# Merging the put-back of expert pairs by token tile, with a new map of scratch places, in a four-layer decoder trunk

## The chip, the cores and the metric

The kernel runs on one core of one Trainium2 chip. The metric is the device time of one launch in microseconds. Every layer of the model is in this one launch.

## What is computed

The input is 256 tokens of 1024 features in float32. Four layers follow each other; layer i takes mixer i mod 3 (short convolution, retention, spatial gating), so layers 0 and 3 have the convolution, layer 1 the retention and layer 2 the gating. After its mixer every layer normalizes, runs the experts, normalizes again, and adds a gated embedding:

```python
for i in range(DEPTH):
    mix = (conv, retention, sgu)[i % 3](x)
    x = _layer_norm(ALPHA * x + mix, ln_g[i, 0], ln_b[i, 0])
    ffn = _moe(x, router_w, router_b, moe_w_gate[i], moe_w_up[i], moe_w_down[i])
    x = _layer_norm(ALPHA * x + ffn, ln_g[i, 1], ln_b[i, 1])
    x = x + sigmoid(x @ ple_w_gate[i] + ple_b_gate[i]) * (p[i] @ ple_w_proj[i])
```

`_moe` picks 2 of 16 experts for each token and sums `combine[:, e] * ((silu(h @ w_gate[e]) * (h @ w_up[e])) @ w_down[e])` over the experts. The expert weights of a layer are 16 x 3 x 1024 x 512 float32, about 100 MB.

## The kernel before

**Two kinds of work for the TensorE.** A dense stage (mixer, gate) multiplies with weights that are split in two parts: a slot of 1 MB (128 partitions x 2048 float32) is loaded into one of six `raw` places, ScalarE writes its high part (`w_hi`, L1249), VectorE the rest (`w_lo`, L1557), and three matmuls use them (L642 to L644). An expert stage multiplies the gathered tokens with unsplit expert weights (L1034).

**The expert stage.** A layer's 16 experts are 8 pairs p of two. Each expert has room for 64 tokens, 32 from each of the two token tiles t. For a pair the TensorE gathers the tokens (L1026), multiplies by four slots of gate weights, four of up and, in the next pair's turn, four of down (`wide`, `down`, 8 matmuls L1034 for a slot). So a layer has 96 loads k of 1 MB in a fixed order (`expert_stream`). Of pair 0 the gate is k 0 to 3 and the up is k 4 to 7. In pair 1 the gate is k 8 to 11; after it come the transpose of pair 0's hidden rows (`turn`), the transpose of its own places (`turn_pick`, L1104) and the gathers for a later pair (`more`), and only then up, k 12 and 13. `more` waits for `place_ready` before its second half. The last load is k 95.

**Put-back.** The outputs of pair p (128 rows: 2 experts x 64 tokens) are evacuated by ScalarE (high part) and VectorE (rest) in `save_y`, one instruction of 128x512 each for either half c of the columns. `put(p)` adds them to the tokens' rows: for each tile t, each half c and both parts one matmul L1044 with the pair's 0/1 matrix `place_of(p)` (`save_place`, VectorE) as weights. That is 8 matmuls a pair and 64 a layer. Pairs 3 to 6 (`LATER`) keep their outputs in places of their own; only the four matmuls of tile 0 run at once, the four of tile 1 at the end (`put_later`), while VectorE already normalizes tile 0. Outputs of the four pairs lie in `w_hi` 1 to 3 and in `xT_hi`.

**The load queue.** All loads of weights are issued by the sync engine in one order that is written out in the code; if one waits, all behind it wait. A dense slot (L479) waits until the slot that was in its place has been used. An expert load (L525) waits in `wait_place`. Expert weights go to any place that is free by then: `expert_places` gives each k a place. There are 22 first places (k 0 to 21), among them the six `raw`, four `high`, four in the arena that the mixers work in (`work`), two `spare`, and `bias`, `norm`, `x`, `y`, `xg`, `emb`. Three of these serve once in a layer (`xg` for k 3, `y` for k 9, `emb` for k 10); the other 19 form a ring: each later k takes the place whose last load is the oldest, and waits for that load's last matmul. So k 22 follows k 0, and from k 30 on a load follows the one 19 before it (k 30 waits for k 11, k 31 for k 12). The ring loses a place when pair 3's outputs need it, and two more with pairs 4 and 5.

`BEHIND` says after which dense slots of a mixer the first expert loads are queued. The keys count the slots from the start of the mixer; the values are numbers of loads. What is not queued there follows after the mixer's last slot. In layer 1 the mixer has 32 slots, in layer 2 it has 36, in the others 16.

```python
BEHIND = [{8: 1, 9: 1, ..., 13: 1, **more} for more in ({14: 2, 15: 3}, {27: 3, 31: 1}, {27: 2, 31: 2, 35: 1})]
```

The norm's parameters lie in `ln_par`, which is the place `norm`; so an expert load can go there only after the first norm of the layer.

## Time and profile before

| | us |
|---|---|
| median of 3 runs | 1613.21 (1612.29 to 1614.31) |
| the profiled execution, its own time | 1616.79 |
| span of the profile, from the first to the last instruction | 1614.9 |
| busy PE (matmul) | 1597.1 (99%) |
| busy DVE (VectorE) | 684.0 (42%) |
| busy ACT (ScalarE) | 460.7 (29%) |
| moved by the weight queue | 530.93 MB, 81.2% of the DMA engines' span |

Busy time is summed over the whole launch. It says nothing on which of two things that run side by side ends last at a given place. The chain of waits and the stretches of time do.

### The profile page before, as it was taken

How to read it: one execution, taken by the hardware profiler on the slowest of the kernel's cores; microseconds unless marked ns; L12 is line 12 of the kernel's file. 1: busy time of each engine (PE TensorE's matmuls, PEld its weight loads, DVE VectorE, ACT ScalarE, POOL GpSimd, SP SyncE). 2: the span in 40 equal slices, each digit the busy share in tenths (PEclk: the TensorE clock that was granted, in tenths of full speed). 3: DMA queues.
4: the chain of work that ended last, by engine and by line, in shares of the span. 5: the costliest groups of instructions: out<-in, count | busy, mean ns of one | idle time of the engine just before them, and what ended most of it. 6: DMA issues, size and time to landing. Idle time of an engine off the chain costs nothing.

```text
span 1614.9 us, 17974 instructions
## 1 busy us (share of the span) xinstructions
PE 1597.1 (99%) x7568; PEld 956.4 (59%) x7568; DVE 684.0 (42%) x1059; ACT 460.7 (29%) x557; POOL 46.2 (3%) x47
## 2 busy tenths in 40 slices
PE   9999999999999999999999999999999999999998
PEld 7874433478877744333788888643434887444335
DVE  5671111294757711111957755511115767211117
ACT  5522111154433221111544433211102552211113
POOL 1000000010000000000110000000010000000000
PEclk9999999999999999999999999999999999999999
DMA  6999999946636799999557556999997388999992
GB/s 260 367 372 407 422 421 420 421 169 264 242 133 242 281 420 421 421 420 421 213 189 293 180 205 235 384 396 421 421 420 327 134 345 369 395 422 421 421 421 100
DMA packets 75146, 534.41 MB, mean 331 GB/s; under 512 B 8976, under 2 KB 9264, under 8 KB 10544
## 3 DMA queue, kind: packets, MB, share of 16 engines
q1 hardware_dynamic: 73728, 530.93, 81.2%
q0 software_dynamic: 1328, 2.21, 0.4%
q8 instruction: 65, 1.06, 0.3%
q14 instruction: 25, 0.20, 0.0%
HBM read 532.06 MB, written 1.05 MB: 330 GB/s over the span
## 4 chain that ended last, share of the span: by engine, by line
PE 88%; DMA 6%; DVE 5%; issue 1%; ACT 1%; SPq 0%; DVEq 0%; ACTq 0%
PE psum L1034 37%; PE psum L642 12%; PE psum L644 12%; PE psum L643 12%; PE psum L1026 4%; DMA raw<-in_experts 4%; PE psum L1044 3%; PE psum L653 3%; DVE w_lo L1557 2%; PE psum L987 2%; DMA x<-in_experts 2%; PE psum L980 1%; PE psum L793 1%; PE psum L932 1%; PE psum L877 1%
## 5 line engine op out<-in xcount | busy, mean ns | idle before, releaser
L1557 DVE TENSOR_TENSOR w_lo<-raw,w_hi 128x2048 fp32r<-128x2048 f32 (+1 forms) x128 | 272.2, 2143 | 191.0 <-ACT w_hi L1249 190.6
L642 PE MATMUL psum<-w_hi,xT_hi 128*128 128x512 f32 x672 | 265.1, 394 | 3.0 <-DVE w_lo L1557 3.0
L1249 ACT ACTIVATE w_hi<-raw 128x2048 fp32r<-128x2048 f32 (+1 forms) x128 | 221.6, 1752 | 160.9 <-PE psum L644 109.8
L644 PE MATMUL psum<-w_hi,xT_lo 128*128 128x512 f32 x672 | 261.8, 390 | 0.0
L643 PE MATMUL psum<-w_lo,xT_hi 128*128 128x512 f32 x672 | 261.6, 389 | 0.0
L1249 ACT ACTIVATE work<-psum 128x512 f32<-128x512 f32 x152 | 85.8, 597 | 344.6 <-PE psum L653 247.3
L642 PEld LDWEIGHTS psum<-w_hi,xT_hi 128*128 128x128 f32 x672 | 126.2, 188 | 30.2 <-DVE w_lo L1557 3.5
L1034 PE MATMUL psum<-raw,xg 128*64 128x512 f32 x624 | 143.8, 594 | 0.0
L644 PEld LDWEIGHTS psum<-w_hi,xT_lo 128*128 128x128 f32 x672 | 126.1, 188 | 26.6
L643 PEld LDWEIGHTS psum<-w_lo,xT_hi 128*128 128x128 f32 x672 | 126.2, 188 | 25.8 <-issue 0.2
L1557 DVE TENSOR_TENSOR work_r<-psum,work_r 128x512 fp32r<-128x512 f32 x52 | 34.5, 688 | 184.9 <-ACT work_r L1249 184.9
L1954 DVE TENSOR_REDUCE cg<-psum 128x1 f32<-128x256 f32 x32 | 13.6, 425 | 233.8 <-PE psum L1104 233.8
L1249 ACT ACTIVATE xg<-psum 128x512 f32<-128x512 f32 x84 | 49.8, 597 | 200.6 <-PE psum L653 102.4
L1034 PE MATMUL psum<-expert_work,xg 128*64 128x512 f32 x448 | 103.5, 594 | 0.0
L1034 PE MATMUL psum<-raw,work 128*64 128x512 f32 x400 | 93.5, 594 | 2.8 <-DMA raw<-in_experts 2.8
L1034 PEld LDWEIGHTS psum<-raw,xg 128*64 128x64 f32 x624 | 43.9, 137 | 84.2 <-issue 83.9
L642 PE MATMUL psum<-w_hi,work_r 128*128 128x512 f32 x224 | 89.3, 398 | 0.8 <-ACT work L1249 0.8
L644 PE MATMUL psum<-w_hi,work_r 128*128 128x512 f32 x224 | 87.6, 391 | 0.0
L643 PE MATMUL psum<-w_lo,work_r 128*128 128x512 f32 x224 | 87.6, 391 | 0.0
L1034 PE MATMUL psum<-expert_high,xg 128*64 128x512 f32 x336 | 79.5, 594 | 0.0
L1557 DVE TENSOR_TENSOR w_hi<-psum,w_hi 128x512 fp32r<-128x512 f32 x24 | 16.6, 692 | 141.6 <-ACT w_hi L1249 141.6
L1249 ACT ACTIVATE work_r<-psum 128x512 fp32r<-128x512 f32 x52 | 29.4, 600 | 161.4 <-PE psum L1034 157.9
(169 smaller groups left out, 1696.9 us busy)
## 6 DMA issues: line engine op xcount, KB each, us to landing
raw<-in_experts SPq DMA_DIRECT2D x128, 1024.0 KB, 16.7
raw<-in_slots SPq DMA_DIRECT2D x120, 1024.0 KB, 4.9
expert_work<-in_experts SPq DMA_DIRECT2D x88, 1024.0 KB, 16.1
expert_high<-in_experts SPq DMA_DIRECT2D x60, 1024.0 KB, 12.6
expert_spare<-in_experts SPq DMA_DIRECT2D x40, 1024.0 KB, 13.7
expert_bias<-in_experts SPq DMA_DIRECT2D x20, 1024.0 KB, 14.5
x<-in_experts SPq DMA_DIRECT2D x20, 1024.0 KB, 16.7
expert_norm<-in_experts SPq DMA_DIRECT2D x16, 1024.0 KB, 14.4
```

The costliest lines, as they stand in the source:

```text
L642: mm(out, lhs[0], rhs[0], start=start, stop=False)
L643: mm(out, lhs[0], rhs[1], start=False, stop=False)
L644: return mm(out, lhs[1], rhs[0], start=False, stop=stop)
L653: last = nc.tensor.transpose(psum[:, bank, i * P:(i + 1) * P], c, ident[:, :])
L793: last = mm(bank, x_whole[:, 2 * at + j, 0:P], w[:, 2 * j + c, :], start=start, stop=stop)
L877: last = mm(psum[:, 4 + k % 4, :], sT[:, h, (c + s) * P:(c + s + 1) * P], rv[:, s, h * DV:(h + 1) * DV], start=s == 0, stop=s == c)
L987: last = mm(psum[:, 2 * t + c, :], pT[:, j, t * P:(t + 1) * P], whole[:, 2 * j + c, :], start=j == 0, stop=j == 1)
L1026: last = mm(rows_of(psum[:, bank, j * SEQ:(j + 1) * SEQ], t, 4), x_split[a][:, t, chunk], pick[:, t, Q * P:(Q + 1) * P], start=a == 0, sto ...
L1034: last = mm(psum[columns(e), bank, :], lhs(j, e), w[:, 2 * j + e, :], start=start and j == 0, stop=stop and j == 1)
L1044: last = mm(psum[:, bank0 + 2 * t + c, :], where[:, t * P:(t + 1) * P], what[i][:, c * NB:(c + 1) * NB], start=start and i == 0, stop=stop ...
L1249: return nc.scalar.activation(dst, src, func)
L1557: return tt(lo, whole, hi.bitcast(F), ALU.subtract)
```

## The change

Pairs 0 and 1, 2 and 3, 4 and 5 are merged two by two. The pair of either parity writes its outputs and its 0/1 rows so that one tensor of 128 rows holds the four experts' 32 rows of tile 0, and another those of tile 1. `put` then runs at odd p only: for pairs 0 and 1 it does both tiles (8 matmuls), for 2 and 3, 4 and 5 tile 0 at once and tile 1 at the end (4 and 4). Pair 6 (4 and 4) and pair 7 (8) stay as they were. The new `save_y` evacuates an even pair whole into both tensors (two instructions where there was one) and an odd pair in four pieces of 32 rows (four where there was one), on ScalarE and on VectorE. The 0/1 matrix of an odd pair is added to that of the even pair by a SCALAR_TENSOR_TENSOR in place of a TENSOR_SCALAR. The two halves of a pair's outputs now use banks 6 and 7, and the TensorE's wait between them goes.

The scratch arrays of the expert stage get a place for each kind of mixer, so that the mixers free other parts of the arena first. `spare` 0 now takes one load of a layer and is then the home of the merged tile 1 outputs. `norm` is free after the layer before; the first norm's parameters go to scratch and are loaded late in the mixer. The load order puts `spare`, `spare`, `norm`, `bias` first, and 13 places instead of 11 (in layer 1 instead of 10) are queued among the mixer's slots. There are still 22 first places; four of them (`spare` 0, `xg`, `y`, `emb`) serve once, so that the ring has 18: k 30 follows k 12 and k 31 follows k 13. Only `high` 1 is taken out of the ring later.

```diff
-LATER = range(3, 7)
-BEHIND = [{8: 1, 9: 1, 10: 1, 11: 1, 12: 1, 13: 1, **more} for more in ({14: 2, 15: 3}, {27: 3, 31: 1}, {27: 2, 31: 2, 35: 1})]
+BEHIND = [{5: 3, 7: 1, 8: 1, 9: 1, 10: 1, 11: 1, 12: 1, 13: 1, 15: 3},
+          {1: 3, 5: 1, 8: 1, 9: 1, 10: 1, 27: 3, 30: 2, 31: 1},
+          {1: 3, 5: 1, 8: 1, 9: 1, 10: 1, 27: 2, 31: 3, 35: 1},
+          {1: 3, 5: 4, 8: 1, 9: 1, 10: 1, 15: 3}]
...
-        ring = [("bias", 0), ("spare", 0), ("spare", 1), raw[4], raw[5], high[0], *early, raw[3], tail[0], raw[0], tail[1], raw[1], tail[2], *late,
-                ("norm", 0), raw[2], ("x", 0)]
...
-        given_up = {high[i + 1]: AT[p, "down", 1] for i, p in enumerate(LATER[:3])}
+        work, xg, y = [("work", i) for i in range(4)], ("xg", 1), ("y", 0)
+        free = [("spare", 0), ("spare", 1), ("norm", 0), ("bias", 0)]
+        dense = [raw[4], raw[5], high[0]]
+        first = [[*free, *work[:3], *dense, xg, work[3], y],
+                 [*free, *dense, *work[:2], xg, *work[2:], y],
+                 [*free, *dense, work[0], xg, *work[1:], y]][layer % 3]
+        order = [*first, raw[3], tail[0], raw[0], tail[1], raw[1], tail[2], raw[2], ("x", 0), ("emb", 0)]
+        n_first = len(order)
+        once = {("spare", 0): 0, xg: EARLY_K, y: LATE_K, ("emb", 0): LAST_K}
+        turns = iter([k for k in range(n_first) if k not in once.values()])
+        loads = [once[place] if place in once else next(turns) for place in order]
+        at = dict(zip(loads, order))
+        ring = [place for place in order if place not in once]
+        last = {at[k]: k for k in loads if at[k] in ring}
+        given_up = {high[1]: AT[4, "down", 1]}
...
+def output_parts(p):
+
+    everything = slice(0, P)
+    if p >= MERGED:
+        return [(everything, 0)]
+    if p % 2 == 0:
+        return [(everything, t) for t in range(T)]
+    return [(slice(CAP * q, CAP * (q + 1)), (q + 1) % 2) for q in range(4)]
...
         def outputs(L, p, t):
+            if p == MERGED:
                 home = xT[0][:, :, :].rearrange("p j n -> p (j n)")
+            elif p > MERGED or t == 0:
+                return scratch[L % 3].y
             else:
-                home = w_hi[:, 1 + LATER.index(p), :]
...
+        def place_of(L, p):
+
+            m = scratch[L % 3]
+            return m.place if p < 2 or p == PAIRS - 1 else m.kept[p // 2 - 1]
...
                 elif kind == "spare":
-                    if L:
+                    if L and i == 0:
+                        sp.wait_ge(ffn_done, T * L)
+                    elif L:
                         sp.wait_ge(experts_used, last_use(L - 1, ("spare", i)))
                 elif kind == "norm":
-                    sp.wait_ge(x_tile_ready, 6 * L + 2)
+                    if L:
+                        sp.wait_ge(x_tile_ready, 6 * L - 2)
                 elif kind == "x":
                     sp.wait_ge(x_lo_ready, T * (L + 1))
...
-                elif L % 3 == 0 and i < 3:
-                    sp.wait_ge(mt_in_psum[L], (4, 4, 8)[i])
+                elif L % 3 == 0 and (kind, i) in (("y", 0), ("work", 3)):
+                    sp.wait_ge(gT_ready[L], 2 * T)
                 elif L % 3 == 0:
-                    sp.wait_ge(conv_ready[L], 1)
-                elif L % 3 == 1 and i >= 2:
-                    sp.wait_ge(o_in_psum, 8)
-                elif L % 3 == 2 and i < 3:
+                    if L:
+                        sp.wait_ge(x_tile_ready, 6 * L)
+                elif L % 3 == 1 and kind == "y":
+                    sp.wait_ge(weights_used, starts[L][0] + 28)
+                elif L % 3 == 1:
+                    sp.wait_ge(*((o_in_psum, 8) if i < 2 else (oT_in_psum, 8)))
+                elif kind == "y":
+                    sp.wait_ge(mt_in_psum[L], 12)
+                elif i < 2:
                     sp.wait_ge(mt_in_psum[L], 4 * (i + 1))
-                elif L % 3 == 1 and i == 1:
-                    sp.wait_ge(weights_used, n)
                 else:
                     sp.wait_ge(weights_used, starts[L][0] + 28)
...
-                    for t in range(1 if p in LATER else T):
+                    for t in range(T if p == 1 else 1):
                         for c in range(2):
-                            last = put_back(place_of(p), outputs(L, p), t, c, p == 0, False)
-                    if p not in LATER:
+                            last = put_back(place_of(L, p), outputs(L, p, t), t, c, p == 1, False)
+                    if p == 1:
                         last.then_inc(put_done, 1)
...
-                    if p == 2:
+                    if p == 3:
                         pe.wait_ge(emb_ready, 4 * (L + 1))
-                    if p > 1:
+                    if p == 1:
+                        pe.wait_ge(xg_ready, gathered(0, 1))
+                    elif p % 2:
                         put(p - 2)
                     else:
-                        pe.wait_ge(xg_ready, gathered(0, 1))
+                        pe.wait_ge(y_ready, 2 * (PAIRS * L + p - 1))
...
-                        pe.wait_ge(y_ready, 2 * (PAIRS * L + p) - 1)
-                        down(p - 1, 1, 6)
+                        down(p - 1, 1, 7)
...
-                    copy(outputs(L, p)[0][:, c * NB:(c + 1) * NB], psum[:, bank, :]).then_inc(y_hi, 1)
+                    for rows, t in output_parts(p):
+                        copy(outputs(L, p, t)[0][rows, c * NB:(c + 1) * NB], psum[rows, bank, :]).then_inc(y_hi, 1)
...
-                    dve.wait_ge(y_hi, 2 * (PAIRS * L + p) + c + 1)
                     cols = slice(c * NB, (c + 1) * NB)
-                    high, low = outputs(L, p)
-                    rest(low[:, cols], psum[:, bank, :], high[:, cols]).then_inc(y_ready, 1)
+                    parts = output_parts(p)
+                    for i, (rows, t) in enumerate(parts):
+                        dve.wait_ge(y_hi, high_parts(L, p, c, i if p % 2 else len(parts) - 1))
+                        high, low = outputs(L, p, t)
+                        last = rest(low[rows, cols], psum[rows, bank, :], high[rows, cols])
+                    last.then_inc(y_ready, 1)
 
...
-                        dve.wait_ge(put_done, 3 * L + 1)
-                    elif p > 5:
-                        dve.wait_ge(put_done, 3 * (L + 1))
-                    ts(place_of(p), psum[:, 6, 0:SEQ], 0.0, None, ALU.is_gt).then_inc(place_ready, 1)
+                    spot = place_of(L, p)
+                    if p == PAIRS - 1:
+                        dve.wait_ge(put_done, L + 1)
+                    if p < MERGED and p % 2:
+                        dve.wait_ge(place_ready, PAIRS * L + p)
+                        stt(spot, psum[:, 6, 0:SEQ], 0.0, spot.bitcast(F), ALU.is_gt, ALU.add).then_inc(place_ready, 1)
+                    else:
+                        ts(spot, psum[:, 6, 0:SEQ], 0.0, None, ALU.is_gt).then_inc(place_ready, 1)
```

## Rows read from the trace of the kernel before

**Rows 1.** The page: busy time by engine, and the GB/s in 40 slices.
```profile
PE 1597.1 (99%) x7568; PEld 956.4 (59%) x7568; DVE 684.0 (42%) x1059; ACT 460.7 (29%) x557; POOL 46.2 (3%) x47
...
GB/s 260 367 372 407 422 421 420 421 169 264 242 133 242 281 420 421 421 420 421 213 189 293 180 205 235 384 396 421 421 420 327 134 345 369 395 422 421 421 421 100
```

**Rows 2.** The chain that ended last: start us, us, what.
```profile
167.58 1.84 PE psum L1044 x8
...
171.60 20.75 PE psum L1034 x96
...
284.89 20.11 DMA raw<-in_experts
...
324.70 1.22 DVE stats L1605 x2
...
739.20 25.32 DMA x<-in_experts
764.56 1.94 PE psum L1034 x8
```

**Rows 3.** A stretch of layer 0: us, busy of each engine, PEclk, DMA share, GB/s.
```profile
134.40:314.90 180.50, 179.57 (x878) 71.83 (x874) 27.45 (x56) 25.06 (x44) 4.93 (x5) 1.00 1.01 418
```

**Rows 4.** The sync queue of layer 0: first start, us to the last's end.
```profile
136.66 11.82 SPq L525 DMA_DIRECT2D expert_work<-in_experts  x4
```

**Rows 5.** Single expert loads (k 31 of layers 0 to 3, then k 20 of layer 1).
```profile
L525 SPq DMA_DIRECT2D expert_work<-in_experts x1: 328/328/328, 148.2 to 148.2; - x1
...
DMA to landing us min/median/max: 6.2/6.2/6.2
...
L525 SPq DMA_DIRECT2D raw<-in_experts x1: 327/327/327, 596.9 to 596.9; - x1
...
DMA to landing us min/median/max: 7.3/7.3/7.3
...
L525 SPq DMA_DIRECT2D expert_work<-in_experts x1: 327/327/327, 1063.3 to 1063.3; - x1
...
DMA to landing us min/median/max: 5.1/5.1/5.1
...
L525 SPq DMA_DIRECT2D expert_work<-in_experts x1: 328/328/328, 1407.0 to 1407.0; - x1
...
DMA to landing us min/median/max: 6.0/6.0/6.0
...
L525 SPq DMA_DIRECT2D raw<-in_experts x1: 328/328/328, 565.0 to 565.0; - x1
...
DMA to landing us min/median/max: 9.1/9.1/9.1
```

**Rows 6.** Layer 2, pair 1: PE and DVE in order of time.
```profile
1061.31 1.94 PE L1034 MATMUL psum<-expert_work,xg 128*64 128x512 f32 x8
...
1059.80 0.41 DVE L1959 TENSOR_SCALAR work_r<-psum 128x256 fp32r<-128x256 f32 x1
```

**Rows 7.** End of layer 1's mixer: PE, sync queue, load of dense slot 31, DVE.
```profile
524.61 1.91 PE L653 MATMUL psum<-const,work 128*128 128x128 f32 x16
...
534.75 0.33 SPq L479 DMA_DIRECT2D raw<-in_slots  x1
...
L479 SPq DMA_DIRECT2D raw<-in_slots x1: 328/328/328, 529.3 to 529.3; - x1
...
DMA to landing us min/median/max: 4.9/4.9/4.9
...
536.77 2.29 DVE L1557 TENSOR_TENSOR w_lo<-raw,w_hi 128x2048 fp32r<-128x2048 f32 x1 [3.15 <-ACT w_hi L1249]
```

**Rows 8.** Late in layer 2's mixer: ACT, DVE and PE in order of time.
```profile
981.77 1.92 ACT L1249 ACTIVATE w_hi<-raw 128x2048 fp32r<-128x2048 f32 x1 [6.27 <-DMA raw<-in_slots]
...
985.93 2.19 DVE L1823 SCALAR_TENSOR_TENSOR work<-psum,const,work 128x384 f32<-128x384 f32 x4
...
989.52 1.91 PE L653 MATMUL psum<-const,work 128*128 128x128 f32 x16
```

More of the change, by code:

```diff
@@ L3 @@
 from concourse import mybir
+from collections import namedtuple
 from contextlib import ExitStack
@@ L108, in expert_places @@
         tail = [("high", HIGH_OF[n - 3 + i]) for i in range(3)]
-        work = [("work", i) for i in range(4)]
-        early, late = {0: (work, []), 1: ([*work[2:], work[0]], [work[1]]),
-                       2: ([work[0], work[1], work[3], work[2]], [])}[layer % 3]
-        ring = [("bias", 0), ("spare", 0), ("spare", 1), raw[4], raw[5], high[0], *early, raw[3], tail[0], raw[0], tail[1], raw[1], tail[2], *late,
-                ("norm", 0), raw[2], ("x", 0)]
-        n_first = len(ring) + 3
-        turns = [k for k in range(n_first) if k not in (EARLY_K, LATE_K, LAST_K)]
-        at = dict(zip(turns, ring))
-        at[EARLY_K], at[LATE_K], at[LAST_K] = ("xg", 1), ("y", 0), ("emb", 0)
-        norm = ring.index(("norm", 0))
-        free = (8, 8, 7)[layer % 3]
-        loads = turns[:free] + [EARLY_K] + turns[free:norm] + [LATE_K] + turns[norm:] + [LAST_K]
-        last = {place: k for k, place in at.items() if k < n_first and place in ring}
-        given_up = {high[i + 1]: AT[p, "down", 1] for i, p in enumerate(LATER[:3])}
+        work, xg, y = [("work", i) for i in range(4)], ("xg", 1), ("y", 0)
[13 more added lines that the diff above has]
+        given_up = {high[1]: AT[4, "down", 1]}
         at_end = [*raw, high[0], *work, ("x", 0)]
@@ L220, in build @@
         w_hi = arena("w_hi", HI, HIGH, SLOT, dt=FR)
-        expert_at = {"work": arena("expert_work", 0, 4, SLOT), "raw": raw, "high": arena("expert_high", HI, HIGH, SLOT),
+        expert_at = {"work": arena("expert_work", 0, 9, SLOT), "raw": raw, "high": arena("expert_high", HI, HIGH, SLOT),
                      "emb": arena("expert_emb", EMB, 1, SLOT), "norm": arena("expert_norm", NORM, 1, SLOT), "bias": arena("expert_bias", BIAS, 1, SLOT),
                      "xg": arena("expert_xg", XT, 2, SLOT),
-                     "spare": sb("expert_spare", 2, SLOT),
-                     "y": arena("expert_y", 6 * SLOT + 2048, 1, SLOT)}
-        w_over = expert_at["work"][:, :, :]
+                     "spare": arena("expert_spare", SPARE, 2, SLOT)}
+        spare_r = arena("spare_r", SPARE, SLOT, dt=FR)
         x = sb("x", T, D)
@@ L321, in rows_of, with high_parts, quad_rows @@
+        def high_parts(L, p, c, i):
+            before = [len(output_parts(q)) for q in range(PAIRS)]
+            return 2 * (L * sum(before) + sum(before[:p])) + c * before[p] + i + 1
+        def quad_rows(v, t):
+            return bass.AP(v.tensor, v.offset + CAP * t, [list(v.ap[0]), [P + CAP * (1 - 2 * t), 2], [HALF, 2], [1, CAP]])
         def rows_of(v, t, experts=2):
             return v.rearrange("p (e h s) -> p h e s", e=experts, h=T)[:, t]
-        pw = view(EX + 5376, SEQ, "p (t n) -> p t n", t=T)
@@ L407, in expert_slot @@
             kind, i = places[L][k]
+            if kind == "y":
+                kind, i = "work", Y_IN[L % 3]
+            elif kind == "work":
+                i = SLOTS_IN[L % 3][i]
             return expert_at[kind][:, i, :]
@@ L532, in _, with load_some @@
                 early = iter(load_order[L])
+                def load_some(behind):
+                    for _ in range(BEHIND[L].get(behind, 0)):
+                        load_expert(L, next(early))
+                if L:
+                    load_some(1)
                 for n in range(n_mixer + (2 if L else 0), n_gate):
                     load(n)
-                    for _ in range(BEHIND[L % 3].get(n - n_mixer, 0)):
-                        load_expert(L, next(early))
+                    load_some(n - n_mixer)
                     if n == QUICK - 1:
@@ L1080, in add_x @@
                     for c in range(2):
[L1081 removed]
+                        for part_of_x in m.x_split:
                             mm(psum[:, 2 * t + c, :], ident_r[:, :], part_of_x[:, t, c * NB:(c + 1) * NB],
```

197 lines of the change are left out of this document (107 added, 90 removed).

## The prediction

> **What bounds the kernel now.** I read the page first. The TensorE is busy for 99% of the span and no other engine for half of it [rows 1], which looks like a kernel that gets shorter by every matmul taken away. The GB/s of the slices speak against that: in the second half of every layer they stand at 420 to 422 [rows 1]. So I asked the chain of waits what ends the expert stages. The reader is to see that it leaves the TensorE near the end of each and follows a DMA: in layer 0 one that was issued at 284.9 and landed at 305.0, in layer 1 the last load of the layer, issued at 739.2 and landed at 764.52; the TensorE's matmuls on it start at 764.56, 0.04 us later [rows 2]. Layers 2 and 3 look like layer 0. The stretch of layer 0 from 134.4 to 314.9 is the proof: 418 GB/s for 180 us, beside a TensorE that is busy for 179.6 of 180.5 us [rows 3]. A load of 1.0486 MB takes 2.51 us at that rate and 2.48 at the page's 422 [rows 1], the 12 of a pair 30 us. The TensorE needs 20.75 us for a pair's 12 slots and 1.84 for a put-back [rows 2], and gathers and transposes come on top, in all less than the DMA does. The two balance only since the first 22 loads are there early. The queue and the TensorE arrive together, so what ends a layer is the landing of load k 95, and the TensorE's time ahead of it is worth nothing unless the loads come earlier too.
>
> So the question is what sets the landing of k 95: the last point at which the load queue stood still, and the number of loads behind it, at 2.48 to 2.51 us each. The sync queue in time shows that point. Four loads, k 28 to 31, are spread over 11.8 us [rows 4], where the DMA needs 10: each waits for the place that it follows, and the queue drains. In layer 2 k 31 is issued at 1063.3, when k 12's matmuls end (1061.31 + 1.94 = 1063.25 [rows 6]), and lands 5.1 us later [rows 5]. That is the time of a load with nothing ahead of it (dense slot 31 took 4.9 [rows 7]). So k 31 was bound by its place there. In layers 0, 1 and 3 it took 6.2, 7.3 and 6.0 us [rows 5], so about 1.2, 2.3 and 1.0 us of queue were still ahead of it. After k 31 nothing waits long: the TensorE uses a slot in 1.73 us (20.75 / 12) and frees places faster than the DMA fills them.
>
> **The change part by part.** *Put-backs.* 64 matmuls L1044 a layer become 40. Eight take 1.84 us [rows 2], so 24 are 5.5 us a layer and 22.1 in all. Of these, 20 a layer lie ahead of k 95 (8 in pair 2's turn, 8 in pair 4's, 4 in pair 6's), where they only make the TensorE wait for the DMA: worth 0. None lies ahead of k 12, so the places for k 30 and k 31 don't come sooner. The other 4 are in the tail, under VectorE, which starts the second tile's statistics at 324.70 [rows 2], when it is done with the first. Between 0 and -0.9 us a layer; I take -0.1 each, since VectorE is on the chain there.
>
> *The ring.* It is the term that decides. k 30 now follows k 12 and k 31 follows k 13. So at the point where the queue has drained there is one load less in it: k 30 lands where k 31 could land at best before, and k 31 comes 2.5 us behind. With 5.0 us for a lone load:
> - layer 0: k 12's end is k 31's old issue, 148.2. k 30 lands at 153.2, k 31 at 155.7; before 148.2 + 6.2 = 154.4. +1.3.
> - layer 1: 596.9 + 5.0 + 2.5 = 604.4; before 604.2. +0.2.
> - layer 2: 1063.3 + 5.0 + 2.5 = 1070.8; before 1068.4. +2.4.
> - layer 3: 1407.0 + 7.5 = 1414.5; before 1413.0. +1.5.
>
> The 64 loads behind k 31 are the same as before, so these 5.4 us go to the ends of the layers. The bounds: with 4.8 us for a lone load 4.6, with 5.1 and a next load 3.0 behind (such unevenness is in the rows: 6.0 us for k 31 in layer 3) 7.8.
>
> *The earlier loads.* Nine of them in all (2, 3, 2, 2) move from the end of the mixer to its middle, where the DMA stands at 133 to 281 GB/s in layer 1 [rows 1]. That would be 9 x 2.49 = 22.4 us. But the loads into `raw` 2, `x` and `emb` stay bound to the end of the mixer, so the queue waits for these, and then for k 1, k 2 and so on of a smaller ring. What is gained ahead of k 30 is lost at k 30. I take 0; the rivals have the other end.
>
> *Dense slots behind more expert loads.* In layer 1 two more loads are queued behind slot 30 and wait for the transposes that end at 524.61 + 1.91 = 526.5 [rows 7]. The queue then holds them until 526.5 + 5.0 + 2.5 = 534.0, and slot 31 lands at 536.5 instead of 529.3 + 4.9 = 534.2. Its high part takes 1.9 and its low part 2.3 us: ready at 540.8 instead of 539.1 [rows 7]. The TensorE has used slot 28 at 534.75 and needs 2.72 us for a tile of a slot (5.45 from 529.3 to 534.75, two tiles), so it comes to slot 31 at 540.2: a stall of 0.6 us. In layer 2 three loads stand behind slot 31 instead of two. The load of slot 32 ends 2.5 us later than 981.8, when ScalarE was waiting for it; VectorE's work on it and then the four gate instructions, 985.93 to 988.1, move to 990.6, and the transposes that need them ran at 989.52 [rows 8]: a stall of 1.1 us. Bounds for either: 0, if the loads overlap better, and 2.5. Together +1.7.
>
> *Evacuations.* Each of ScalarE and VectorE gets 2 more instructions for an even pair and 6 for an odd one. A piece of 32 rows has the same 512 columns; no row shows one, so its cost lies between next to nothing and the whole; 256 columns took 0.41 us [rows 6] and 384 took 2.19 / 4 = 0.55 [rows 8], which makes 0.69 for 512, and I take that for either engine. That is 24 x 0.69 = 16.6 us more a layer on VectorE, which is busy for 27.45 of 180.5 us [rows 3]. The last of an odd pair's pieces ends some 3.5 us after the pair's last down slot (five instructions in a row, one ScalarE's and four VectorE's), the `hidden` behind it 0.75 later; the TensorE comes to `turn` after one up slot and four gate slots, 5 x 1.73 = 8.6 us. So it is hidden, with 4 us to spare. If it weren't, the TensorE's 4.6 us of new slack in each layer would cover the first of it.
>
> *The 0/1 matrix.* In pair 1 it lies ahead of k 12: the TENSOR_SCALAR of 0.41 us [rows 6] becomes a SCALAR_TENSOR_TENSOR, at least 0 and at most 0.3 us dearer, behind one more wait. I take 0.07 each, +0.3. The first norm's parameters now come in the mixer, some 8 us behind their release and more than 10 ahead of the norm: 0. The wait that was taken from the TensorE ahead of the second down half idled no matmul: 0.
>
> Sum: 5.4 + 1.7 + 0.3 - 0.4 = +7.0 us on the span of 1614.9 and on the profiled execution's own 1616.79. That execution is 3.6 us above the median; the change of time is the same for both, so 1613.2 + 7.0 = 1620.2. It is 0.43%, more than the 0.2% (3.2 us) below which a measurement of this kernel can't tell it from no change.
>
> **The rivals.** *The matmuls pay.* If the TensorE set the ends, 22.1 us would go: 1591. For it speaks the 99% [rows 1], against it the last load's landing 0.04 us ahead of its use [rows 2]. "Perfetto Trace Analysis" of the Trainium skill (section on identifying the most-contended engine) warns that matmul busy time isn't a measure of how close the TensorE is to its limit, and otherwise tells to optimize the engine with the highest occupancy first; by occupancy alone the sum would be this rival's, and the rows on the last load decide against it. 5%.
>
> *The prefetch pays: faster.* It decides if k 22 to 30 find their places free. In layer 1 `raw` 2 was loaded at 565.0 and landed 9.1 us later [rows 5] since two others were ahead; alone it lands at 570.0, and 4.1 us stay won if the ring doesn't take them back. In the other layers fewer loads lay behind it; I put 1 to 2 us on each. About 8 less 1.7 of stalls: 1607. Against it: k 12's end plus 5 us. 12%.
>
> *Nothing measurable.* The 64 loads behind k 31 take 160.3 us in layer 1 (596.9 + 7.3 to 764.52 [rows 2, 5]), where 64 x 2.48 are 158.7. If such small gaps close everywhere, four layers give back up to 6.4 us: 1614. For it: the gaps have no cause that I can name. 18%.
>
> *Evacuations late.* If a piece costs more than I take, or a wait between VectorE's pieces of different rows is dear, `turn` comes late by more than 4 us in three pairs of a layer. Beyond the TensorE's slack of 4.6 us that gives some 2 us a layer more: 1628. 8%.
>
> **How the numbers follow.** My forecast (1615 to 1625 by its bounds) has 57%. With 10% or so between and outside the cases, the range that holds 8 in 10 is 1608 to 1626. Faster by over 0.2% is 0.17, within it 0.20, slower 0.63.
>
> **What would show it.** In the profile after: 160 matmuls L1044 instead of 256, and no fewer us on the chain; the last expert loads of the layers landing 1.2 to 4 us later within their layers, each a few hundredths ahead of its matmuls; TensorE waits on `in_experts` of some 4 to 6 us a layer; k 30 issued at the end of k 12's matmuls and landing about 5 us later; a TensorE stall near the last mixer slots of layers 1 and 2. I am wrong if k 95 lands earlier in its layer than before, or if the TensorE waits for VectorE at `turn`.

## The result, and the profile of the changed kernel

The changed kernel took 1620.88 us (median of 6 runs, 1618.82 to 1624.03) beside 1614.03 us of the kernel before on the same chip (6 runs, 1612.29 to 1615.29): a ratio of 1.0043, interval 1.0033 to 1.0054. It is slower by 6.9 us, where +7.0 was forecast. In a later job it took 1623.31 us beside 1614.20, ratio 1.0052 (1.0038 to 1.0066). The total came out as forecast, but the terms did not: two were too small, and shorter stretches that I had not foreseen made up for them. Two executions of the experiments below, one of ring_back (1808.66 us) and the profiled one of ring_two_less (2742.35 us), ran at a mean granted clock of 0.849 and 0.554; they are in no ratio and move the medians by no more than 0.2 us.

The page of the changed kernel, the lines that answer to [rows 1]:

```profile
PE 1582.4 (98%) x7472; PEld 936.1 (58%) x7472; DVE 744.3 (46%) x1155; ACT 514.6 (32%) x653; POOL 45.6 (3%) x47
GB/s 364 333 321 366 422 421 421 421 273 258 183 139 243 292 349 423 421 421 421 309 229 203 180 202 259 327 391 422 420 421 410 244 266 302 341 423 420 422 420 104
PE 82%; DMA 12%; DVE 4%; ACT 1%; issue 1%; SPq 0%; POOL 0%; DVEq 0%; ACTq 0%; POOLq 0%
```

The TensorE is busy for less time, the second half of every layer still stands at 420 to 423 GB/s (one slice at 410), and 12% of the chain is DMA, where it was 6%. The chain at the end of layers 0 and 1, start, us, what (it answers to [rows 2]):

```profile
281.67 25.22 DMA expert_work<-in_experts
306.89 0.04 issue
306.94 1.94 PE psum L1092 x8
...
731.77 25.76 DMA expert_high<-in_experts
757.53 0.04 issue
757.58 1.94 PE psum L1092 x8
...
767.50 1.94 PE psum L1092 x8
769.44 2.17 PE psum L1102 x8
```

The matmuls on layer 1's k 95 start at 767.50, 0.04 us behind its landing at 767.46, as before. That is 2.94 us later than the 764.56 of [rows 2]; 2.17 of it is there when the layer's experts start, 0.77 comes in the layer. What the TensorE waited for (us, times, longest) says the same; "L1092" is the expert products:

```profile
PE psum L1092 <- DMA expert_work<-in_experts: 10.7, 20, 1.4
PE psum L1092 <- DMA raw<-in_experts: 7.1, 14, 0.6
PE psum L1092 <- DMA expert_high<-in_experts: 2.9, 5, 0.7
PE psum L699 <- DVE w_lo L1621: 2.2, 4, 1.4
```

20.7 us of waits for expert loads in four layers, 5.2 a layer; in the trace of before the waits for expert loads come to 3.9. The put-backs are 160 matmuls instead of 256, 5.5 us a layer less; 4.6 of these lie ahead of k 95, and 4.2 us a layer are found again in these rows as waiting. And the ring in layer 2, k 30 and k 31, the load queue's issues and the time to landing of each (to hold against k 31 in [rows 5]):

```profile
L572 SPq DMA_DIRECT2D expert_work<-in_experts x1: 328/328/328, 1064.2 to 1064.2; - x1
...
DMA to landing us min/median/max: 5.3/5.3/5.3
...
L572 SPq DMA_DIRECT2D expert_work<-in_experts x1: 328/328/328, 1065.9 to 1065.9; - x1
...
DMA to landing us min/median/max: 6.7/6.7/6.7
```

k 30 leaves when k 12's matmuls end and lands at 1069.4, k 31 at 1072.6; before, k 31 had landed at 1068.4. The layer's experts start 0.9 us later than before, so within the layer k 31 is 3.3 us late.

To see where the time goes I cut each layer in three: the experts (first matmul on k 0 to the first on k 95), tail and gate (from there to the first product of the next mixer), and the mixer with routing (from there to the next k 0). The table has the differences to the trace of before, worked out from these starting points. Two things in it are told in the last section: a "gap" is a stretch in which the TensorE stands still behind the put-backs, a "fall" one of 3.4 us at half the granted clock.

| us against before | experts, layers 0 to 3 | sum | tails and gates | start and mixers of layers 1 to 3 | span |
|---|---|---|---|---|---|
| changed | 2.35, 0.77, 2.32, 2.41 | 7.9 | -4.9 | -0.5, 1.75, -0.8, 0.3 | +3.6 |
| changed_again | 2.27, 1.01, 3.03, 1.30 | 7.6 | -4.9 | -0.2, 5.3, -0.5, 0.1 | +7.4 |
| ring_one_less | 1.39, 0.66, 1.78, 1.72 | 5.6 | -0.6 | 0.2, 0.0, -1.4, 0.0 | +3.7 |
| ring_back | -0.28, -1.56, -0.36, -0.36 | -2.6 | -1.1 | -0.6, 2.2, 0.5, -0.6 | -2.1 |
| ring_back_dense_first | -1.00, -1.21, -0.35, -0.38 | -2.9 | -0.9 | -0.4, 0.0, 0.9, -0.5 | -3.9 |
| merge_2_to_5 | -0.96, -1.43, -0.74, -0.48 | -3.6 | -4.9 | -0.6, 0.8, -0.7, -0.5 | -9.4 |
| more_matmuls | 3.45, 2.25, 3.34, 2.62 | 11.7 | -2.6 | -0.5, 1.15, 0.4, -0.6 | +9.5 |
| more_matmuls_later | 1.27, 0.40, 2.65, 3.40 | 7.7 | -3.4 | -0.3, 3.9, 1.8, -0.5 | +9.3 |
| e5_norm_in_mixer | -0.81, 0.01, 0.35, -1.29 | -1.7 | -3.2 | 0.6, 0.0, -0.7, 0.0 | -5.0 |
| e7_dense_first | 1.77, 2.16, 1.99, 1.75 | 7.7 | -4.9 | -0.5, 0.0, 0.9, 0.4 | +3.6 |

A profiled execution is one draw. That of before was 2.8 us above its median of 1614.03, so the first trace's +3.6 and the runs' +6.9 do not contradict each other; one fall of the clock, in before's trace and not in the changed one's, is 1.7 of it. The changed kernel's two traces agree to 0.3 us on the sum of the expert stages, but single layers differ by up to 1.1, so a single layer's figure says little.

### The profile page after: what moved, and what is told of

The parts are those of the page before. It is cut to its first block, busy times and chain, and to the rows that moved or that the text cites. A ratio compares the mean times of both kernels' runs of the same rounds, so it can differ in the third digit from the quotient of the medians.

```text
span 1618.5 us, 17946 instructions
## 1 busy us (share of the span) xinstructions
PE 1582.4 (98%) x7472; PEld 936.1 (58%) x7472; DVE 744.3 (46%) x1155; ACT 514.6 (32%) x653; POOL 45.6 (3%) x47
## 4 chain that ended last, share of the span: by engine, by line
PE 82%; DMA 12%; DVE 4%; ACT 1%; issue 1%; SPq 0%; POOL 0%; DVEq 0%; ACTq 0%; POOLq 0%
PE psum L1092 32%; PE psum L699 11%; PE psum L701 11%; PE psum L700 11%; DMA expert_work<-in_experts 7%; DMA expert_high<-in_experts 5%; PE psum L1084 4%; PE psum L710 3%; PE psum L1044 2%; PE psum L850 2%; DVE w_lo L1621 1%; PE psum L1102 1%; PE psum L1037 1%; PE psum L989 1%; PE psum L934 1%
## 5 line engine op out<-in xcount | busy, mean ns | idle before, releaser
L1621 DVE TENSOR_TENSOR w_lo<-raw,w_hi 128x2048 fp32r<-128x2048 f32 (+1 forms) x128 | 267.7, 2108 | 189.2 <-ACT w_hi L1310 188.8
L1092 PE MATMUL psum<-raw,xg 128*64 128x512 f32 x704 | 165.0, 595 | 4.0 <-DMA raw<-in_experts 3.5
L1621 DVE TENSOR_TENSOR work_r<-psum,work_r 128x512 fp32r<-128x512 f32 (+1 forms) x100 | 67.6, 688 | 183.0 <-ACT spare_r L1310 98.8
L1092 PE MATMUL psum<-expert_work,xg 128*64 128x512 f32 x512 | 119.3, 596 | 6.7 <-DMA expert_work<-in_experts 6.7
L1092 PEld LDWEIGHTS psum<-raw,xg 128*64 128x64 f32 x704 | 48.7, 137 | 102.7 <-issue 87.5
L1310 ACT ACTIVATE work_r<-psum 128x512 fp32r<-128x512 f32 (+1 forms) x100 | 57.7, 594 | 155.5 <-PE psum L1092 150.7
L1092 PEld LDWEIGHTS psum<-expert_work,xg 128*64 128x64 f32 x512 | 35.3, 137 | 80.4 <-issue 65.8
L1092 PE MATMUL psum<-expert_high,xg 128*64 128x512 f32 x320 | 76.0, 595 | 3.2 <-DMA expert_high<-in_experts 1.8
L1092 PE MATMUL psum<-raw,work 128*64 128x512 f32 x320 | 75.5, 594 | 3.6 <-DMA raw<-in_experts 3.6
## 6 DMA issues: line engine op xcount, KB each, us to landing
expert_high<-in_experts SPq DMA_DIRECT2D x68, 1024.0 KB, 16.6
```

Of the source, the lines that this page charges most:

```text
L1092: last = mm(psum[columns(e), bank, :], lhs(j, e), w[:, 2 * j + e, :], start=start and j == 0, stop=stop and j == 1)
L1310: return nc.scalar.activation(dst, src, func)
L1621: return tt(lo, whole, hi.bitcast(F), ALU.subtract)
```

## Experiments: the ring

**ring_one_less and ring_two_less**, the ring's length alone, in the kernel before:

```diff
         given_up = {high[i + 1]: AT[p, "down", 1] for i, p in enumerate(LATER[:3])}
+        given_up["spare", 0] = 0
```

> The kernel before, and spare 0 isn't used again after its first load, so the ring is one place shorter. Nothing else. Theory: k 30 follows k 12, k 31 follows k 13, and the last loads land 1.3, 0.2, 2.4 and 1.5 us later within their layers: +5.4 us, between 4.6 and 7.8, so 1619.4 (1618.6 to 1621.8). Rival (small gaps behind k 31 take it up): within 2 us of 1614.0.

Measured: 1622.50 us beside 1613.61, ratio 1.0058 (1.0043 to 1.0073), +8.9, which is above the expected range. Its trace has the expert stages 1.39, 0.66, 1.78 and 1.72 us longer, 5.6 in all, against 5.4 forecast; its profiled execution was the fastest of its six. The rest of the +8.9 lies outside what the trace shows. k 30 of layer 2 (in the four layers it took 4.8 to 5.1 us, the 5.0 of the forecast):

```profile
L526 SPq DMA_DIRECT2D expert_work<-in_experts x1: 328/328/328, 1062.4 to 1062.4; - x1
...
DMA to landing us min/median/max: 4.8/4.8/4.8
```

> The kernel before with spare 0 and spare 1 both out of the ring after their first load: the suspected cost doubled. Theory: every place past the first costs one whole load of 2.5 us in each layer, since nothing is left in the queue that could cover it: 5.4 + 4 x 2.5 = +15.4 us, 1629.4, between 1627 and 1633. Rival (each place costs the same as the first): +10.8, 1624.8. Rival (gaps take it up): under 1618.

Measured: 1631.55 us, ratio 1.0105 (1.0090 to 1.0119), +17.9. It lies in the expected range. There is no trace at the normal clock. The second place costs 9.1 us more, near the 10 of a whole load in each layer. By the runs the first cost as much (8.9), by its trace 5.6.
**ring_back**, the changed kernel with the place back in the ring:

```diff
-        once = {("spare", 0): 0, xg: EARLY_K, y: LATE_K, ("emb", 0): LAST_K}
+        once = {xg: EARLY_K, y: LATE_K, ("emb", 0): LAST_K}
...
-    if p >= MERGED:
+    if p >= MERGED or p < 4:
         return [(everything, 0)]
```

> The changed kernel with only pairs 4 and 5 merged: pairs 0 to 3 put both tiles back from y at once, so spare 0 holds no output and is again in the ring (k 30 follows k 11 and k 31 follows k 12, as in the kernel before). All else is as changed, the earlier loads, the scratch places and the norm's place too. It has 16 put-back matmuls a layer more than the changed kernel (56 instead of 40). Theory (the ring sets the last load's landing): the expert stages get back the 7.9 us that they lost, the 64 added matmuls cost nothing: 1620.9 - 7.9 = 1613, between 1611 and 1615. Rival (the matmuls pay): 64 x 0.23 = 14.7 us slower than the changed kernel, 1635. Rival (neither counts): 1621.

Measured: 1615.08 us beside 1613.61, ratio 1.0005 (0.9996 to 1.0014). It has 64 put-back matmuls more (80 more ahead of the last loads, 16 fewer behind them; the expected range ended at 1615) and is 5.8 us faster than the changed kernel. The expert stages went from +7.9 to -2.6: 10.4 us came back, more than the 7.9 expected. The TensorE waited 0.6 us for expert loads instead of 20.7. But 5.4 us appeared elsewhere, in two gaps:

```profile
PE psum L714 <- issue: 5.4, 2, 2.7
...
PE psum L1090 <- DMA expert_work<-in_experts: 0.6, 2, 0.3
```

**merge_2_to_5**: which place is taken, and from when.

```diff
-        given_up = {high[1]: AT[4, "down", 1]}
+        given_up = {high[1]: AT[2, "down", 1], high[2]: AT[4, "down", 1]}
...
-                home = spare_r[:, :] if p < 4 else w_hi[:, 1, :]
+                home = w_hi[:, p // 2, :]
```

> The changed kernel with pairs 2 to 5 merged and pairs 0 and 1 not: the second tile's output of pairs 2 and 3 lives in w_hi 1, given up by the ring at k 39, that of pairs 4 and 5 in w_hi 2, given up at k 63; spare 0 is in the ring. 48 put-back matmuls a layer (the changed kernel 40, the one with pairs 4 and 5 alone merged 56, the kernel before 64). The ring is as long as before at k 30 and k 31 and gets shorter only where the TensorE frees places faster than they are filled. Theory: what matters is only where the ring gets shorter: 1614 to 1615.5, the same as with pairs 4 and 5 alone merged (1615.1). Rival (every place taken costs, wherever): 1618 to 1621. Rival (8 matmuls fewer a layer than with 4 and 5 alone pay): 1609.

Measured: 1608.06 us beside 1614.20 (6 and 17 runs), ratio 0.9962 (0.9950 to 0.9974): faster than both kernels, and near the 1609 of the rival that I had written down last. The rival's mechanism isn't what the trace shows. The expert stages are only 1.0 us shorter than ring_back's, where the 48 put-backs fewer ahead of the last loads would be 11.0. The rest is 3.7 us in the tails and gates, where the gaps of ring_back aren't, and 2.6 us in the mixers. The ring that gets shorter at k 39 and k 63 doesn't slow the loads: from the landing of k 31 to that of k 95 they take 160.5 us a layer, beside 160.7 in ring_back and in the kernel before. A place taken from k 22 on made the expert stages 5.6 us longer in ring_one_less, where nothing else was changed, and 7.9 in the changed kernel: that is the clearest statement of what was wrong with the change.

```profile
PE psum L1090 <- DMA expert_work<-in_experts: 4.7, 9, 0.5
...
PE psum L1090 <- DMA raw<-in_experts: 1.6, 3, 0.6
...
PE psum L1090 <- DMA expert_high<-in_experts: 1.1, 2, 0.6
```

## Experiments: what a matmul is worth

**more_matmuls** and **more_matmuls_later**, the changed kernel with 20 matmuls a layer added (the second version has `2 <= p <= 6`):

```diff
                     pe.wait_ge(silu_ready, PAIRS * L + p)
+                    if p <= 5:
+                        for i in range(4):
+                            mm(psum[:, 4, :], m.x_split[0][:, 0, 0:P], m.x_split[0][:, 0, 0:NB], start=i == 0, stop=i == 3)
```

> The changed kernel with 20 matmuls a layer added ahead of the gate products of pairs 1 to 5 (4 each, the shape and type of a put-back, into the bank that the gate product then starts anew): as many as the change took away ahead of k 95. Theory: they fall into the TensorE's waits for loads: within 1 us of the changed kernel's 1620.9. Rival (the matmuls pay): 80 x 0.23 = +18.4 us, 1639. Rival (half pays, since the TensorE has only 4.2 to 4.6 us of lead a layer, which 4.6 us use up whole): +1 to +4.

Measured: 1627.86 us, ratio 1.0091 (1.0077 to 1.0105), 7 us over the changed kernel: neither 0 nor 18.4. The trace showed my mistake. Four of the 20 lie ahead of k 12, and k 30 waits for k 12's end. In every layer k 30 is issued 31.6 us behind the first matmul on k 0 instead of 30.3, 1.3 us later (not the 0.92 of four put-backs, which the next expectation takes). The expert stages are 3.8 us longer in all than the changed kernel's, so some 1.3 of these 5.1 us are made up again behind k 30. The TensorE's waits for expert loads fell from 20.7 to 5.3 us. The same experiment without these four:

> The changed kernel with the same 20 added matmuls a layer, but ahead of the gate products of pairs 2 to 6 instead of 1 to 5, so that none lies ahead of k 12. The trace of the first version showed its expert stages 3.8 us longer than the changed kernel's in all four layers together, and its k 12 ended 0.9 us (four matmuls) later in each, and two gaps of 1.9 us behind the branch that follows the experts, which it has no part in. Theory: the four matmuls ahead of k 12 paid 4 x 0.92 = 3.7 us by way of the ring, the 16 others nothing; now the expert stages are as long as the changed kernel's (within 1 us in sum), and the time is 1620.9, between 1619.5 and 1623. Rival (the lead of the TensorE is used up, so that added matmuls pay from some count on): as slow as the first version, 1627.9.

Measured: 1625.49 us, ratio 1.0065 (1.0053 to 1.0077). The expert stages are what theory said, 7.7 us over before as against 7.9 and 7.6 of the changed kernel: 80 matmuls, 18.4 us of TensorE time, cost nothing there. The time of the whole is above the range all the same (changed_again, in the same job: 1623.31). Its trace has two gaps of 3.3 us together behind the branch and two falls of the clock, and the changed kernel's first trace has neither.

**e6_before_light** and **e6_after_light**, both kernels with less to load, so that the DMA is no longer the bound. Every fourth load from k 35 on, 16 a layer, brings 64 of its 2048 columns; the kernels leave out the rest of these weights and compute something else in the same number of instructions:

```diff
-                sp.dma_start(expert_slot(L, k), A["experts"][L, p, ROW[part] + i]
+                n = 64 if k > 31 and k % 4 == 3 else SLOT
+                sp.dma_start(expert_slot(L, k)[:, 0:n], A["experts"][L, p, ROW[part] + i, :, 0:n]
```

> The kernel before with less to load: from k 32 on every fourth expert load brings 64 of its 2048 columns, so that 16 slots a layer keep mostly the weights that their place had; the output is another, and the branch for crowded experts is never taken. Theory: the DMA has 38 us a layer to spare, the TensorE sets the ends; since it was busy for 99% of the span it gains only its few waits: 1608 to 1613. Rival (the DMA was far ahead as the bound): under 1600.

> The changed kernel with the same loads left short. Theory: with the TensorE as the bound the 20 put-backs a layer ahead of k 95 pay in full, 4 x 4.6 = 18.4 us, and the ring costs nothing; with the gate stages' -4.6 and the mixers' +2.8 it is 20 us faster than the light kernel before, about 1591 (1588 to 1595). Rival (the evacuations, now with less cover, take it back): within 8 us of the light kernel before. Rival (put-backs are hidden in any case): within 3 us of it.

Measured: 1607.92 (ratio 0.9964, 0.9952 to 0.9976) and 1592.92 us (0.9878, 0.9862 to 0.9893), 15.0 us apart. In neither trace does the TensorE wait for an expert load. The expert stages differ by 4.1 us in each of the four layers (16.4 in all), beside 18.4 for the 80 put-backs; the rest is a new wait for ScalarE of 0.47 us in each layer (1.9 in all), told below. So the put-backs are real work, and it is the loads that kept it from being seen. The same traces price the loads: without their bound the expert stages are 6.3 us shorter in the kernel before and 30.6 in the changed one. The 24.3 us between are the 16.4 that the change saved the TensorE and the 7.9 by which it made the loads later. (The waits listed by row, 3.9 and 20.7 us, are only part of these sums.) On the chain of the light changed kernel (the page's shares by engine) DMA is 2%, and that is dense slots:

```profile
PE 92%; DVE 5%; DMA 2%; ACT 1%; issue 0%; SPq 0%; DVEq 0%; ACTq 0%
```

## Experiments: the smaller terms

**e5_norm_in_mixer**, the kernel before with the first norm's parameters fetched where the changed kernel does (`load_norm(L, 0)` behind `conv_ready`, `o_in_psum` or slot 32 of the mixer, and no longer behind the layer ahead).

> The kernel before with one edit: in layers 1 to 3 GpSimd fetches and broadcasts the first norm's parameters in the mixer, where the changed kernel does, and no longer in the gate stage of the layer ahead, where the broadcast of 2.29 us ran beside VectorE's low parts (6.45 us for two; 4.48 in the changed kernel). Theory: the gate stages of layers 0 to 2 get shorter as they did in the changed kernel (by 1.3, 1.1 and at least 1.0 us), and little is lost in the mixer: -3.4 us, 1610.6, between 1609 and 1613. Rival (the time is VectorE's alone and hidden, the shorter gate stages come from the other scratch places): within 1 us of 1614.0.

Measured: 1613.32 us beside 1613.89, ratio 0.9995 (0.9986 to 1.0005): by the runs, no difference. The trace does show the effect. Layer 0's gate stage, first in the kernel before (GpSimd, then VectorE: start, us), then in e5_norm_in_mixer:

```profile
333.12 2.29 POOL L589 PARTITION_BROADCAST ln_par<-ln_par  x1 [1.39 <-DMA ln_par<-in_ln_b]
...
330.98 6.45 DVE L1557 TENSOR_TENSOR w_lo<-raw,w_hi 128x2048 fp32r<-128x2048 f32 x2
```

```profile
330.77 4.49 DVE L1562 TENSOR_TENSOR w_lo<-raw,w_hi 128x2048 fp32r<-128x2048 f32 x2
```

With the broadcast beside it VectorE needs 1.96 us more for the two, the TensorE waits 0.9 us for the second, and tails and gates of layers 0 and 1 get 1.2 and 1.1 us shorter without it, as in the changed kernel. It isn't a fixed price: in ring_one_less layer 0's broadcast started 2.4 us behind the first low part instead of 2.1, was itself stretched to 4.2 us, and the TensorE didn't wait. Two traces that have the broadcast in its old place are as short there in layer 0: the tails and gates of layers 0 and 1 are 1.2 and 0.5 us shorter than in before's trace in ring_one_less, and 1.5 and 0.0 in e6_before_light. So before's trace was a costly draw, and the usual price is below its 2.3 us, which fits the runs' -0.6. Layer 2's -0.9 is the gap behind the branch, 0.9 us here and 1.8 in before. The profiled execution was one of the fast ones of its eleven.

**e7_dense_first**, the changed kernel with the dense slots ahead of the extra expert loads:

```diff
-          {1: 3, 5: 1, 8: 1, 9: 1, 10: 1, 27: 3, 30: 2, 31: 1},
-          {1: 3, 5: 1, 8: 1, 9: 1, 10: 1, 27: 2, 31: 3, 35: 1},
+          {1: 3, 5: 1, 8: 1, 9: 1, 10: 1, 27: 3, 31: 3},
+          {1: 3, 5: 1, 8: 1, 9: 1, 10: 1, 27: 2, 31: 2, 35: 2},
```

> The changed kernel with another order in the load queue: in layer 1 the two expert loads behind dense slot 30 go behind slot 31, in layer 2 one of the three behind slot 31 goes behind slot 35 (as in the kernel before). Theory: the stall at layer 1's last mixer slot (+1.6 us in the changed kernel's trace) goes, in layer 2 0.4 us; nothing is lost at k 30, which waits for k 12 in any case: -2.0 us, 1618.9, between 1617.5 and 1620. Rival (the ring's point is a load's count behind the stall, and what the mixer gains the experts wait for): 1620.9, within 0.7.

> The kernel with pairs 4 and 5 alone merged and spare 0 in the ring, and the dense slots of layers 1 and 2 loaded ahead of the extra expert loads as in the other run of that order: the best that these edits add up to. In the changed kernel that order alone gained nothing that could be told from zero (1620.2), since what layer 1's mixer gained its expert stage lost. Theory (the DMA's own rate between k 22 and k 31 takes it back): 1615, within 1 us of the kernel without it. Rival (with the longer ring the gain of 1.6 us in the mixer stays): 1613, no slower than the kernel before.

Measured: 1620.19 us, ratio 1.0044 (1.0027 to 1.0061): no gain that can be told from none. The stall of layer 1's mixer is gone (0.0 instead of 1.75), but its expert stage is 1.4 us longer. k 30 left 2.3 us earlier, at 596.8, but needed 6.8 us to land instead of 4.9, and k 31 landed at 607.5 as in the changed kernel (607.6). With the longer ring, in ring_back_dense_first, the gain stays: 1612.71 us, ratio 0.9989 (0.9980 to 0.9998), 2.4 us less than ring_back (in another job; each against its own before: -1.5 and +1.5), and layer 1's mixer and experts together are 1.9 us shorter than ring_back's. That rival was right.

**changed_again**:

> The changed kernel once more, as it is: a second profiled execution and more times. Theory: 1620.9 within 1 us; the expert stages 2.4, 0.8, 2.3 and 2.4 us longer than before as in the first trace; a gap of up to 2.8 us behind the branch after layer 2's or layer 3's experts may be there or not, since its place in the code is the same in all kernels and it was there in five of nine traces. Rival (that gap belongs to particular kernels): none, as in the first trace.

Measured: 1623.31 us, above the 1 us that I allowed. Expert stages +7.6 as against +7.9. No gap again, so my guess that the gap falls on any kernel by chance gets no support; two traces can't rule it out.

## Why the prediction was right, and where it wasn't

- **What bounds the kernel: shown.** The last load of each layer is used 0.04 us behind its landing, 80 added matmuls leave the expert stages as long as they are, and with lighter loads the same put-backs pay 4.1 us a layer.
- **The ring: right in its mechanism, too small, and partly right by luck.** +5.4 forecast, +7.9 and +7.6 in the two traces of the changed kernel; the ring alone gave +5.6. The forecast had two steps, k 31 lands later and k 95 lands later by as much. The landings, counted from the first matmul on k 0 of their layer and set against before, show both steps off:

| us later than before | layers 0 to 3 | sum |
|---|---|---|
| forecast, k 31 and k 95 alike | 1.3, 0.2, 2.4, 1.5 | 5.4 |
| changed, k 31 | 3.9, 1.2, 3.3, 2.8 | 11.2 |
| changed, k 95 | 2.4, 0.8, 2.3, 2.4 | 7.9 |
| changed_again, k 31 | 2.8, 1.5, 5.0, 1.4 | 10.6 |
| changed_again, k 95 | 2.3, 1.0, 3.0, 1.3 | 7.6 |
| ring_one_less, k 31 | 1.8, 0.3, 2.5, 1.8 | 6.5 |
| ring_one_less, k 95 | 1.4, 0.7, 1.8, 1.7 | 5.5 |

  The issue was foreseen to a hundredth: k 30 leaves 30.35 us behind the first matmul on k 0, where k 31 left before. What was mis-sized is "5.0 + 2.5" behind it. In ring_one_less k 30 took 4.8 to 5.1 us in each layer; in the changed kernel's two traces 4.8 to 7.6, and k 31 landed 2.4 to 3.9 us behind it. The load ahead of it, k 29, was late too: in layer 0 it left at 143.1 and landed at 150.5, though the DMA moved only 193 to 254 GB/s from 146 to 150; why it did not run faster stays open. The ring of the changed kernel is one place shorter from k 22 on and holds up k 22 to 29 as well. I took the point where the queue drains from the kernel before and kept it where it was. The other step erred the other way: the 64 loads behind k 31 were to take as long as before, and took 3.4 and 3.0 us less in the four layers. That is the mechanism of the rival "nothing measurable", and it took up a quarter to a third of the loss.
- **The earlier loads: 0, as forecast.** Within its layer the embedding's load k 10 landed 1.9, 4.4, 0.7 and 1.6 us earlier, and nothing of it was left at k 29, which landed 0.4 to 3.2 us later than before. With the longer ring (ring_back) the expert stages end up 2.6 us shorter than before, so there the prefetch, or the matmuls, did pay a little.
- **Dense slots: mis-sized.** Layer 1's last slot was to stall the TensorE for 0.6 us. It was 1.4 us in one trace and 1.9 in the other, and in the second the clock fell twice in this mixer, which makes it +5.3. Layer 2's forecast of 1.1 was 0 at the place, where the transposes run 174.9 us behind the mixer's start as before; 16 us later the TensorE waited 0.3 and 0.6 us for a low part. In ring_back and the two kernels with added matmuls the wait at the place was there, 0.9 us. e7_dense_first takes the stall away, and the experts take most of the gain.
- **The 0/1 matrix: 0** instead of 0.3: SCALAR_TENSOR_TENSOR 414 ns, TENSOR_SCALAR 414 ns, and k 12's matmuls end at the same point of the layer as before.
- **Evacuations: hidden by the loads, and priced about right.** A piece of 32 rows costs as much as one of 128: 0.684 us on VectorE, 0.587 on ScalarE, 0.69 forecast for both. VectorE is busy for 15.1 us more a layer (16.6 forecast). The TensorE doesn't wait for VectorE at `turn`, but once in each layer for ScalarE, 0.47 us, which it didn't before (all kernels with merged pairs have this wait, the kernel before hasn't); the loads cover it, and in e6_after_light it is paid. Form by form (us, mean ns):

```profile
L1621 DVE TENSOR_TENSOR spare_r<-psum,spare_r 32x512 fp32r<-32x512 f32 x32 | 21.9, 684 | 83.0 <-ACT spare_r L1310 82.8
...
L1310 ACT ACTIVATE spare_r<-psum 32x512 fp32r<-32x512 f32 x32 | 18.8, 587 | 73.6 <-PE psum L1092 73.2
```

- **What I missed: the gate stages, -4.9 in both traces.** I had put the moved norm parameters at 0 since they come in time, and didn't ask what the broadcast had done where it was taken from: -1.2 and -1.1 in layers 0 and 1 by the trace of e5_norm_in_mixer, less by its runs. In layer 2 the kernel before has a gap of 1.8 us behind the branch, and the changed one none. Both are set against one trace of before in which they happened to be costly, so the -4.9 is more than the change itself gives. The 0.8 us left of it hold the tail put-backs, -0.4 forecast; they can't be told apart.
- **The sum.** Forecast +7.0. The two traces give +3.6 and +7.4. Without the 1.7 us that each fall of the clock costs (one in before, none and two in the changed kernel) they are +5.3 and +5.7, beside +6.9 and +9.1 by the medians (+8.4 by the second ratio). Between 1.6 and 3.4 us stay without a name. That the total was right to 0.1 us is luck: an undersized loss stood against a missed gain, and the next job's total was 2 us off.

## What to carry to other kernels

In a kernel that streams through a ring of places, look for the load at which the queue runs dry: a place taken ahead of it costs up to a whole load each time the kernel passes there (here 1.4 to 2.3 us a layer, a load being 2.5), and a place taken behind it cost nothing that could be seen. Work taken from an engine that waits at the end of a stage is worth nothing until the loads come earlier, so pair such a saving with the one that moves the loads. And price a moved step at both ends, also by what runs better where it was.

## What the runs showed that I had not expected

**The clock falls behind some stalls, and without any.** In changed_again the TensorE waited 1.93 us for the low part of dense slot 31, and 1.1 us behind it the granted clock fell from full (2.4 GHz) to half (1.2 GHz). TensorE in order of time, then the windows (us; busy of each engine; granted clock, DMA share, GB/s):

```profile
542.66 0.50 PE L699 MATMUL psum<-w_hi,work_r 128*128 128x512 f32 x1 [1.93 <-DVE w_lo L1621]
543.00 0.40 PE L700 MATMUL psum<-w_lo,work_r 128*128 128x512 f32 x1
...
544.03 0.63 PE L701 MATMUL psum<-w_hi,work_r 128*128 128x512 f32 x1
544.45 0.63 PE L699 MATMUL psum<-w_hi,work_r 128*128 128x512 f32 x1
```

```profile
541.00:544.00 3.00, 1.34 (x5) 1.10 (x6) 1.60 (x1) 0.00 (x0) 0.00 (x0) 0.96 0.11 44
544.00:546.00 2.00, 2.00 (x6) 1.58 (x5) 1.27 (x2) 0.00 (x0) 0.00 (x0) 0.50 0.00 0
546.00:548.00 2.00, 2.00 (x7) 1.57 (x7) 0.82 (x3) 0.00 (x0) 0.00 (x0) 0.70 0.00 0
```

It lasted 3.4 us, in which matmuls started 0.43 us apart instead of 0.23; half of it, 1.7 us, is lost. In the first trace the wait was 1.4 us and the clock stayed. The profiled execution of the kernel before had one such fall too, in layer 2's routing, where its TensorE had no wait:

```profile
1024.00:1026.00 2.00, 2.00 (x9) 1.30 (x9) 0.95 (x7) 0.54 (x2) 0.00 (x0) 0.68 1.06 446
1026.00:1028.00 2.00, 2.00 (x3) 0.66 (x2) 1.93 (x11) 0.00 (x0) 0.00 (x0) 0.50 0.96 397
```

Of the other traces e7_dense_first and ring_back had one within the span, ring_back_dense_first and more_matmuls_later two, the others none but at the very end. So there are nine falls in all. Three begin about 1 us behind a wait of 1.9, 2.7 and 2.9 us; the other six have no wait above 0.12 us in the 12 us ahead of them, and waits of 2.0, 2.4, 2.7 and 3.1 us had no fall behind them. That a stall brings a fall is therefore not shown. The executions' mean clocks differ as such falls would make them (the changed kernel: 1620.40 us at 1.000, 1621.36 at 0.998, 1624.03 at 0.996), but not every difference goes that way (1618.92 at 0.999), so the falls explain a part of the scatter.

**A gap behind the branch.** Behind the last put-back the TensorE passes the branch for crowded experts. In layers 2 and 3 some kernels stand still there for 0.9 to 3.1 us with nothing that the profile can name: before 1.8 (one gap), e5_norm_in_mixer 0.9, ring_one_less 2.4, more_matmuls 3.5 (two), more_matmuls_later 3.3 (two), ring_back 5.4 (two), ring_back_dense_first 6.0 (two). The changed kernel in both traces, e7_dense_first, merge_2_to_5 and the two light kernels have none.

```profile
PE psum L659 <- issue: 1.8, 1, 1.8
```

That is the row of before. The kernels without it either let the TensorE wait for loads late in the layer or have little to load there, but ring_one_less waits too and has it. Its cause stays open, and with it some 4 us of the difference between ring_back and merge_2_to_5; an experiment on the branch alone was not made. One rival is the loading of instructions. In all traces but the two light ones the DMA queue of the kind "instruction" moves a piece of 16 KB, in 0.9 to 1.3 us, within 2 us of this place in every layer, whether there is a gap or not; in the two light ones, which have no gap, none is that near. That alone doesn't make a gap, but it may be a condition of it.
